# A two-layer encoder step on one core: stacked index queries, and attention and retention steps put in another order

## What is computed

```
qi = rope(qi) * IDX_DIM ** -0.5                      # 16 index heads of 64
s_idx = einsum('bqhd,bsd->bqhs', qi, ki)
s_idx = einsum('bqhs,bqh->bqs', relu(s_idx), wi)
sel   = top_k(where(admissible, s_idx, -inf), topk)
p = softmax(s); o = einsum('bqcgs,bqscd->bqcgd', p, v_sel)
# retention, per head, chunk by chunk
o = einsum('bihd,bjhd->bhij', q, k) * decay
o = einsum('bhij,bjhe->bihe', o, v) + einsum('bihd,bhde->bihe', q, s) * inter
od = rmsnorm(o, g_dn) * silu(dg)
```

## Time and profile before

| | us |
|---|---|
| median of 3 runs (2869.24 to 2869.51) | 2869.35 |
| the profiled execution | 2871.04 |
| its span, first to last instruction | 2869.1 |
| PE busy with matmuls in the span | 2851.2 |
| DVE, ACT, POOL busy | 1428.7, 1070.8, 186.4 |

### The profile page before, as it was taken

One profiled execution on the slowest core, in us unless ns is written; L12 is line 12 of the kernel. 1 busy time (PEld: TensorE's weight loads), 2 busy tenths in 40 slices (PEclk: granted clock), 3 DMA queues, 4 the chain that ended last, 5 costly groups with the idle time before them and its releaser, 6 DMA issues.

```text
span 2869.1 us, 45023 instructions
## 1 busy us (share of the span) xinstructions
PE 2851.2 (99%) x18666; PEld 2806.6 (98%) x18666; DVE 1428.7 (50%) x1546; ACT 1070.8 (37%) x1236; POOL 186.4 (6%) x112
## 2 busy tenths in 40 slices
PE   9999999999999999999999999999999999999999
PEld 9997799999999999999999999899999999999999
DVE  7677645543443343344466774546444443444443
ACT  5334533332332233233335633434333333333332
POOL 2000002000000000000221241112000000000000
PEclk9999999999999999999999999999999999999999
DMA  6433024444444444444444444244444444444443
GB/s 232 138 114 110 30 89 140 143 143 140 146 141 141 145 140 141 145 140 141 145 148 155 152 148 148 95 162 147 149 153 147 154 147 152 150 149 153 147 152 136
DMA packets 112783, 405.25 MB, mean 141 GB/s; under 512 B 12656, under 2 KB 14752, under 8 KB 112480
## 3 DMA queue, kind: packets, MB, share of 16 engines
q1 hardware_dynamic: 108864, 392.64, 41.1%
q0 software_dynamic: 1616, 6.31, 0.6%
q10 hardware_dynamic: 2128, 3.66, 0.3%
HBM read 396.48 MB, written 6.09 MB: 140 GB/s over the span
## 4 chain that ended last, share of the span: by engine, by line
PE 97%; DVE 2%; ACT 1%; issue 0%; DMA 0%; ACTq 0%; DVEq 0%
PE PS L1411 31%; PE PS L1416 30%; PE PS L1415 30%; PE PS L1490 0%; ACT pr L483 0%; DVE pr L910 0%; DVE w_lo L843 0%; PE PS L1691 0%; DVE rb L1052 0%; PE PS L1488 0%; PE PS L1866 0%; PE PS L1474 0%; ACT w_hi L435 0%; PE PS L1738 0%; PE PS L1737 0%
## 5 line engine op out<-in xcount | busy, mean ns | idle before, releaser
L843 DVE TENSOR_TENSOR w_lo<-stage,w_hi 128x1024 fp32r<-128x1024 f32 x734 | 920.3, 1256 | 1197.0 <-ACT w_hi L435 1196.6
L435 ACT ACTIVATE w_hi<-stage 128x1024 fp32r<-128x1024 f32 x740 | 784.6, 1061 | 1634.3 <-PE PS L1416 1624.9
L1411 PE MATMUL PS<-xh,w_hi 128*128 128x336 f32 (+1 forms) x3264 | 1025.1, 314 | 1.0 <-DVE kk L1087 0.6
L1416 PE MATMUL PS<-xh,w_lo 128*128 128x336 f32 (+1 forms) x3248 | 1017.1, 313 | 0.0
L1415 PE MATMUL PS<-xl,w_hi 128*128 128x336 f32 (+1 forms) x3248 | 1015.6, 313 | 0.0
L1411 PE MATMUL PS<-hh,w_hi 128*128 128x336 f32 (+1 forms) x2032 | 635.7, 313 | 0.0
L1416 PE MATMUL PS<-hh,w_lo 128*128 128x336 f32 (+1 forms) x2032 | 635.0, 313 | 0.0
L1415 PE MATMUL PS<-hl,w_hi 128*128 128x336 f32 (+1 forms) x2032 | 634.1, 312 | 0.0
L1411 PEld LDWEIGHTS PS<-xh,w_hi 128*128 128x128 f32 x3264 | 613.1, 188 | 3.5 <-issue 1.1
L1415 PEld LDWEIGHTS PS<-xl,w_hi 128*128 128x128 f32 x3248 | 612.5, 189 | 0.4
L1416 PEld LDWEIGHTS PS<-xh,w_lo 128*128 128x128 f32 x3248 | 610.0, 188 | 0.0
(11 more groups left out here) (343 smaller groups left out, 1529.1 us busy)
## 6 DMA issues: line engine op xcount, KB each, us to landing
stage<-in_wstream SPq DMA_DIRECT2D x740, 512.0 KB, 3.3
out_s<-so POOLq DMA_DIRECT2D x8, 256.0 KB, 2.8
x<-in_x_in SPq DMA_DIRECT2D x6, 336.0 KB, 7.1
out_y<-x ACTq DMA_DIRECT2D x3, 672.0 KB, 3.9
dmask<-in_ret POOLq DMA_DIRECT2D x4, 352.0 KB, 5.7
stage<-in_wstream SPq DMA_DIRECT2D x4, 256.0 KB, 3.7
s<-in_s_in POOLq DMA_DIRECT2D x1, 1024.0 KB, 6.2
x<-in_x_in SPq DMA_DIRECT2D x4, 168.0 KB, 3.9
```

What stands on the lines that cost most here:

```text
L435: act.activation(w_hi[:, s, :], stage[:, s, :], ACT.Copy).then_inc(hi_ready, 1)
L843: dve.tensor_tensor(w_lo[:, s, :], stage[:, s, :], w_hi[:, s, :].bitcast(F32), ALU.subtract).then_inc(lo_ready, 1)
L1411: pe.matmul(out, wh, rh, start=first, stop=False)
L1416: mm = pe.matmul(out, wl, rh, start=False, stop=last)
```

## The change

- **Index.** A head's 64 rows of rounded query and the rest of them now lie over each other in one 128-row tile (`qeven`, `qodd`). The keys' rounded part is in all rows, so one pass gives both products, and a second gives rounded query by low key: two passes, not three. ACT rounds into both tiles (four copies of 128x1344, two before), DVE writes the rest over the other head's rows (eight instructions of 32x1344, two of 128x1344 before).
- **Query projection.** The copy out of four banks becomes four copies of one bank, and PE waits for each by itself. The sums of squares start with the part of `sqq` that is there first.
- **Attention.** `pta` and `ptb` are both copied by ACT, ahead of the exponentials of the step. `mol` comes a step later. DVE makes the weights of heads 0 and 1 before it copies the sums. Half of a key unit moves ahead of the transposes of head 6.
- **Retention.** Outputs alternate between banks 6, 7 and 1, 2 (`out_bank`), squares between `osq` and `osq2`. DVE makes the decay mask before it waits for the root. ACT's rounding of output h - 1 (`round_output`) comes after the copies for head h + 1.

The core of the diff:

```diff
-        qih = place("qih", [P, 8, T], B + 20 * TB, F32R)
+        qeven = place("qeven", [P, 8, T], B + 20 * TB, F32R)
+        qodd = place("qodd", [P, 8, T], B + QI * TB, F32R)
         kph = place("kph", [P, 2, KEYS], B + 16 * TB, F32R)
...
+
+        def squares_of(h):
+            return osq2 if h % 2 else osq
+
+
+        def out_bank(h):
+            return 1 if h % 2 else 6
...
+                    if g0 == 0 and s == 8:
+                        softplus_input()
+                        act.wait_ge(qb_taken, 1)
+                        act.activation(sdq[0:8], sdq[0:8], ACT.Sqrt, bias=gcol("eps", rows=slice(0, 8))
+                                       ).then_inc(qb_sd, 1)
+                    if 2 <= s < 10:
+                        g = g0 + s - 2
+                        act.wait_ge(pt_psum, g + 1)
+                        if g >= 2:
+                            act.wait_ge(o_psum, g - 1)
+                        act.activation(pta[:, g % 2], PS[:, pb, :].rearrange("p (a b) -> p a b", a=4),
+                                       ACT.Copy).then_inc(pta_ready, 1)
+                        act.activation(ptb[0:80, g % 2, 0:80], PS[0:80, pb + 1, 0:80], ACT.Copy)
+                        act.activation(ptb[NS_TOK:80, g % 2, 80:T], PS[NS_TOK:80, pb + 1, 80:T],
+                                       ACT.Copy).then_inc(ptb_ready, 1)
...
-                    if 2 <= s < 10:
-                        g = g0 + s - 2
-                        act.wait_ge(pt_psum, g + 1)
-                        if g >= 2:
-                            act.wait_ge(o_psum, g - 1)
-                        act.activation(pta[:, g % 2], PS[:, pb, :].rearrange("p (a b) -> p a b", a=4),
-                                       ACT.Copy).then_inc(pta_ready, 1)
...
-                if (g, j) in ((2, 8), (3, 8)):
-                    act.wait_ge(qi_turned, g - 1)
-                    act.activation(qih[:, 4 * g - 8:4 * g - 4, :], zt4[:, g - 1], ACT.Copy).then_inc(qih_ready, 1)
...
+                for q, c, at_ in ((qeven, 0, (2, 8)), (qodd, 0, (2, 8)), (qeven, 1, (3, 8)), (qodd, 1, (3, 9))):
+                    if (g, j) == at_:
+                        act.wait_ge(qi_turned, c + 1)
+                        act.activation(q[:, 4 * c:4 * c + 4, :], rb4[:], ACT.Copy).then_inc(qih_ready, 1)
...
+            def round_output(h):
+                act.wait_ge(od_ready, h + 1)
+                act.activation(moh[:, 8 + 2 * h:10 + 2 * h, LIVE], z2[:, DG + 2 * h:DG + 2 * h + 2, LIVE],
+                               ACT.Copy).then_inc(doh_ready, 1)
...
                     tokens_first(h + 1)
+                if h:
+                    round_output(h - 1)
                 act.wait_ge(oms_psum, h + 1)
...
-                act.wait_ge(od_ready, h + 1)
-                act.activation(moh[:, 8 + 2 * h:10 + 2 * h, LIVE], z2[:, DG + 2 * h:DG + 2 * h + 2, LIVE],
-                               ACT.Copy).then_inc(doh_ready, 1)
+            round_output(3)
...
+                def weights(g):
+                    dve.wait_ge(p_ready, g + 1)
+                    ch.link(dve.reciprocal(rsum[:, g % 3, :], rsum[:, g % 3, :]))
+                    for q in range(3):
+                        seg = pr[:, g % 3, SEG[q]:SEG[q + 1]]
+                        e = dve.tensor_scalar(seg, seg, rsum[:, g % 3, q:q + 1], None, ALU.mult)
+                    e.then_inc(pn_ready, 1)
+
+                for s in range(8 + 4):
                     if s < 8:
...
+                    if 1 <= s < 9 and (g0, s) != (0, 2):
+                        weights(g0 + s - 1)
                     if g0 == 0 and s == 1:
+                        weights(1)
                         dve.wait_ge(qb_ms, 1)
-                        dve.tensor_copy(sdq[0:8], PS[0:8, 4:6, 0:T]).then_inc(qb_taken, 1)
-                    if 2 <= s < 10:
-                        g = g0 + s - 2
-                        dve.wait_ge(pt_psum, g + 1)
-                        if g >= 2:
-                            dve.wait_ge(o_psum, g - 1)
-                        dve.tensor_copy(ptb[0:80, g % 2, 0:80], PS[0:80, pb + 1, 0:80])
-                        dve.tensor_copy(ptb[NS_TOK:80, g % 2, 80:T], PS[NS_TOK:80, pb + 1, 80:T]).then_inc(ptb_ready, 1)
-                    if g0 == 0 and s == 9:
+                        dve.tensor_copy(sdq[0:8, 1], PS[0:8, 5, 0:T])
+                        dve.wait_ge(qb_ms, 2)
+                        dve.tensor_copy(sdq[0:8, 0], PS[0:8, 4, 0:T]).then_inc(qb_taken, 1)
+                    if s >= 4:
...
-                    if s >= 3:
-                        g = g0 + s - 3
-                        dve.wait_ge(moh_ready, g + 1)
-                        dve.tensor_tensor(mol[:, h0 + s - 3, :], PS[:, ob + g % 2, 0:T],
-                                          moh[:, h0 + s - 3, :].bitcast(F32),
-                                          ALU.subtract).then_inc(mol_ready, 1)
...
+                        dve.tensor_tensor(rb4[:], q4, rb4[:], ALU.add).then_inc(qi_turned, 1)
+
+                for c, odd, r, at_ in ((0, 0, 0, (2, 9)), (0, 0, 64, (2, 9)), (0, 1, 32, (2, 10)), (0, 1, 96, (2, 10)),
+                                        (1, 0, 0, (3, 9)), (1, 0, 64, (3, 10)), (1, 1, 32, (3, 11)), (1, 1, 96, (4, 4))):
+                    if (g, j) == at_:
+                        dve.wait_ge(qi_turned, c + 1)
+                        dve.wait_ge(qih_ready, 2 * c + 1 + odd)
+                        q8 = (qeven, qodd)[odd][:, 4 * c:4 * c + 4, :]
+                        to = r + 32 - 64 * odd
+                        dve.tensor_tensor(q8[to:to + 32], rb4[r:r + 32], q8[r:r + 32].bitcast(F32),
+                                          ALU.subtract).then_inc(qstack_ready, 1)
...
+                    ch.link(dve.tensor_tensor(kpl[:], kpad[:, 0:2, :], kph[:].bitcast(F32), ALU.subtract))
+                    dve.tensor_tensor(kph[:, 0], kph[:, 0].bitcast(F32), kph[:, 1].bitcast(F32),
+                                      ALU.add).then_inc(kpl_ready, 1)
...
-                if (g, j) == (7, 8):
+                if (g, j) == (7, 9):
...
-                    dve.tensor_copy(qb[:, 4 * c:4 * c + 4, :], PS[:, 4:8, 0:T]).then_inc(qkv_evac, 1)
+                    for o in range(4):
+                        dve.tensor_copy(qb[:, 4 * c + o, :], PS[:, 4 + o, 0:T]).then_inc(qkv_evac, 1)
...
+                if h < 3:
+                    decayed_scores(h + 1)
                 dve.wait_ge(osd_ready, h + 1)
                 ch.link(dve.reciprocal(osd[:, LIVE], osd[:, LIVE]))
-                if h < 3:
-                    decayed_scores(h + 1)
...
-                                qh, ql = qih[:, h // 2, t0:t0 + P], qil[:, h // 2, t0:t0 + P]
-                                pe.matmul(out, qh, kph[:, h % 2, k0:k1], start=True, stop=False)
-                                pe.matmul(out, qh, kpl[:, h % 2, k0:k1], start=False, stop=False)
-                                mm = pe.matmul(out, ql, kph[:, h % 2, k0:k1], start=False, stop=True)
+                                q_ = (qeven, qodd)[h % 2][:, h // 2, t0:t0 + P]
+                                pe.matmul(out, q_, kph[:, 0, k0:k1], start=True, stop=False)
+                                mm = pe.matmul(out, q_, kpl[:, h % 2, k0:k1], start=False, stop=True)
...
+                def bank_free(o):
+                    pe.wait_ge(qkv_evac, 4 * c - 3 + o)
...
-                pe.wait_ge(qb_sq, 3)
+                pe.wait_ge(qkv_evac, 10)
+                pe.wait_ge(qb_sq, 1)
...
+                    pe.wait_ge(qb_sq, 2 + j // 4)
...
-                   lambda s: keys_b(0) if s == 9 else None)
+                   lambda s: keys_b(0, range(2)) if s == 8 else None,
+                   lambda s: keys_b(0, range(2, 4)) if s == 9 else None)
...
+                if h >= 2:
+                    pe.wait_ge(on_ready, 2 * h - 2)
+                tb = out_bank(h)
...
-                    pe.wait_ge(on_ready, 2 * h)
-                else:
+                if h == 0:
                     pe.wait_ge(s0_in_s, 16)
+                pe.wait_ge(ktok_ready, h + 1)
                 pe.wait_ge(qd_ready, h + 1)
                 pe.wait_ge(pT_ready, h + 1)
...
```

More of the change, by code:

```diff
@@ L268, in build @@
         osd = place("osd", [P, T], B + 17408 + 2 * TB)
+        osq2 = place("osq2", [P, 2, T], A + 14 * TB)
         PS = ctx.enter_context(nc.psum_tensor("PS", [P, 8, 512], F32))
@@ L499, in attend @@
                                        ACT.Copy).then_inc(moh_ready, 1)
-                    if g0 == 0 and s == 8:
-                        softplus_input()
-                        act.wait_ge(qb_taken, 1)
-                        act.activation(sdq[0:8], sdq[0:8], ACT.Sqrt, bias=gcol("eps", rows=slice(0, 8))
-                                       ).then_inc(qb_sd, 1)
             def mlp(n, u_mlp, g_mlp, L, whole, ahead=None):
@@ L798, in _ @@
                 act.wait_ge(do_psum, h + 1)
-                act.activation(osq[:, :, LIVE], PS[:, 1:3, LIVE], ACT.Square).then_inc(osq_ready, 1)
+                b = out_bank(h)
```

(26 more changed lines are left out.)

76 lines of the change are left out of this document (35 added, 41 removed).

## The result

| | before | after |
|---|---|---|
| median of 10 runs, us | 2869.45 (2868.83 to 2870.89) | 2876.85 (2875.03 to 2879.09) |
| the profiled execution | 2871.04 | 2876.41 |
| its span | 2869.1 | 2874.6 |
| mean granted clock | 0.999 | 0.998 |
| PE busy with matmuls | 2851.2 | 2848.1 |

The changed kernel is 7.4 us slower by the medians, 0.26%; the ratio of the two is 1.002, with an interval of 1.0012 to 1.0028. So it is slower, by somewhat more than the 0.2% (5.7 us) that the prediction named as the least that can be told from no change. The forecast was 2873.5 with a range of 2865 to 2879.

A forecast was written before the change was run, and what follows sets the result against it. The prediction took PE to bound the kernel, busy 2851.2 of 2869.1 us. Index +1.9, attention A -4.2, attention B -1.3, retention +4.5 and clock +3.3 sum to +4.2 on 2869.35, so 2873.5 us, range 2865 to 2879.

The forecast's parts named there:

- two waits of 4.7: Retention, h = 1 and h = 2: PE idles 4.7 us from the transposes' end to the squares, +9.4 together.
- The rival without the stall: Retention: the sample state is read in time, term -4.9 instead of +4.5, two dips go, 2860.8; chance 0.13.
- The 0.2 that the sum adds to each wait for refilling: Attention and retention: each removed wait of PE also saves about 0.2 us in which PE's queue refills.
- a period falls from 5.85 to about 5.73: Index stage: the time from one pair of heads to the next shrinks only this far; six periods save 0.7 us.
- if PE's own work were the limit. It is not: Index stage: the loop outside PE limits the pairs, so the 5.7 us of matmuls saved over eight pairs isn't won.
- The rival of cheap subtractions and a limit at PE's work: Index stage: pairs shorten by their full 0.71, 32-row subtractions cost 0.4: -5.7 instead of +1.9, 2865.9; chance 0.12.
- a new wait of 3.3: Attention of A: the first transposes start where they did, so time saved ahead becomes some 3.3 us of PE waiting.
- the 4.2 of the sum: Attention of A: values of head 7 come 4.2 us earlier, 3.9 of waits plus 0.8 of refill less 0.5.
- the 0.45 of the sum: Attention of A, step 8: root and table load, 1.28 us, stand ahead of a `pta`; 0.45 of that is not covered.
- I take the two longest: Clock: of four new idle stretches (4.7, 4.7, 3.3, 2.9 us), two are followed by half clock, +3.3 us.
- took off 1.7 for the dip of before: Retention: the half-clock stretch behind the first wait for `osq` in the kernel before goes, -1.7 us.
- slower, by the clock: Rival: every long idle is followed by the 1.2 GHz level, two dips more, +3.4, so 2876.9; chance 0.33.

The follow-up runs named there:

- b_idx: Kernel before with only the index part of the change, the stacked index queries: 2872.03 us, ratio 1.0005.
- b_two_passes: Kernel before with two passes of the index scores, leaving out low query by rounded key: 2867.41 us, ratio 0.9988.
- b_att: Kernel before with only the parts of the change in query projection and attention: 2864.98 us, ratio 0.9983.
- b_one_pass: Kernel before with one pass of the index scores, rounded query by rounded key: 2864.70 us, ratio 0.9982.
- b_ret: Kernel before with only the retention part of the change: 2879.91 us, ratio 1.0033.
- idx_subs_behind: Changed kernel with the 32-row subtractions behind the additions of their step instead of ahead: 2873.37 us.
- att_weights_behind: Changed kernel with the weights of head 1 behind DVE's two copies of the sums of squares: 2875.18 us.
- ret_low_later: Changed kernel with DVE's low part of output h - 1 behind the sample state and decay mask of head h: 2864.15 us, ratio 0.9975.
- all_three: Changed kernel with DVE's low part later, subtractions behind additions, head 1's weights behind the copies, and ACT's last query rounding ahead of the ReLUs: 2855.78 us, ratio 0.9947.

## Why the prediction was right, and where it was not

The measured time lies in the range, but outside the 2869 to 2876 that the forecast kept for itself: +7.4 is in the part that was called slower, with a chance of 0.35. The waits and the order behind them came as described. Two errors on the clock, both the same way, make the rest, and that the number stayed in the range owes something to the width of the range.

- **Retention, the wait.** Forecast: two waits of 4.7 through copies, rounding, `mol` and `so`. Measured: 4.57 each, in that order, and 4.6 with the part alone. Moving one DVE instruction took both away. The rival without the stall, 0.13, is out. The 0.2 that the sum adds to each wait for refilling, for which it shows no row, comes out too: 13.5 us less in the stage for 13.1 of waits and half clock, and 0.19 behind the wait of pair 2 (7.53 between the pairs, less 5.07 and 2.27).
- **Index stage.** Forecast +1.9, measured +1.7, with 2.3 and 2.8 of new waits where 2.1 (by the start of pair 2) and 2.9 were expected. Of the 1.7, 0.3 lies ahead of pair 0, which starts at 116.93 and not 116.66, after a wait of 0.6 for `xl` at 13.8 us, far ahead of the stage; from pair 0 on it is +1.5, in `b_idx` too. Two sizes inside were off and cancelled, which is luck: chunk 4 came 3.5 late and not 2.9, and the pairs behind it gave back 1.8 and not 1.0, since the loop's period was put at 5.73 and is 5.48 on the mean. The step "a period falls from 5.85 to about 5.73" took one pass through the loop for the steady state. And "if PE's own work were the limit. It is not" holds for the changed kernel only: in the kernel before PE had no wait for `rt`, and its own work filled the 5.85. The price of the 32-row subtraction, 1.55, was exact, so the number of rows does not count in it:

```profile
124.65 1.55 DVE L1128 TENSOR_TENSOR qeven<-rb,qeven 32x1344 fp32r<-32x1344 f32 x1
```

  The rival of cheap subtractions and a limit at PE's work, -5.7, is out; of its saving in PE's work about half came (3.0 of 5.7 in `b_two_passes`).
- **First transposes.** Forecast: they start where they did before, a new wait of 3.3. Measured: 283.17, which is 281.44 plus the 1.7 that the index stage brought, and a wait of 2.8.
- **The steps of attention.** From first transposes to the values of head 7 it was 31.66 us and is 28.84, less by 2.8. With the half-clock stretch of 282.8 to 286.2 in it (some 1.5 of matmul time) that is 4.3 against the 4.2 of the sum. Mixer B gave 1.5 against 1.3. Two rows of ACT in the changed kernel, the table load ahead of the root and the two `ptb` copies, show the sizes:

```profile
303.95 1.28 ACT L490 ACT_TABLE_LOAD   x1
305.25 0.85 ACT L490 ACTIVATE sdq<-sdq,gains 8x672 f32<-8x672 f32 x1
...
306.49 0.21 ACT L499 ACTIVATE ptb<-PS 80x80 f32<-80x80 f32 x1
306.71 0.37 ACT L500 ACTIVATE ptb<-PS 16x256 f32<-16x256 f32 x1
```

  The copies are 0.6 together, where 0.8 was taken between 0.5 and 1.2. The load with its root ends at 306.10, and PE waits 0.57 for `ptb` of that step, against the 0.45 of the sum. The root starts 0.02 behind the load; the drain of the Trainium skill (ScalarE: Activation LUTs, section What ACT_TABLE_LOAD costs) shows neither in the rows nor in the wait.
- **The clock was mis-sized.** The sum took two dips, +3.3. The profile has four lengths of the dip of the earlier trace rows at the 1.2 GHz level, 3.4 + 6.8 + 3.4 = 13.7 us; less the 2.7 in which PE stood idle anyway (282.8 to 283.2, 1825.6 to 1827.7, 1846.1 to 1846.3), half of the rest is 5.5 us. The step "I take the two longest" failed twice: the first wait of retention was followed by two lengths, and the wait of 2.8 by one.
- **And it was booked against the wrong number.** The sum took off 1.7 for the dip of before and carried the result to the median. But the profiled execution of before was 1.7 above the median because of that dip, and the profiles of `b_idx`, `b_att` and `b_one_pass`, with the same retention code, have none there. Without it before's profile would stand at 2869.3, where the median is. The executions of before beside the experiments say the same: the 36 with a granted clock of 1.000 have medians of 2869.4 to 2869.6 in the three series, the 30 with 0.999 have 2871.4 to 2872.1. So the median's execution most likely has no dip, and there was nothing to take off. Without any dip before's span would be 2869.1 - 1.7 = 2867.4 and the changed kernel's 2874.6 - 5.5 = 2869.1: +1.7 from waits and matmuls (the sum's own terms without clock are 1.9 - 4.2 - 1.3 + 9.4 - 3.2 = +2.6), and +5.5 from the clock. These make +7.2, against the +7.4 of the medians.
- So the median landed on the number of the rival "slower, by the clock" (2876.9, chance 0.33), though not by its book, and that is luck as well: it wanted one dip behind each of four waits, and the profile has none in the index stage.

The Trainium skill (TensorE: Matmul & The Clock Gate, section HAM oscillation — how this bites in real kernels) has a PE put back to half clock by a long wait between bursts of matmuls, so that the next burst starts cold. The runs agree for the longest waits: in the changed kernel, in `b_ret`, `idx_subs_behind` and `att_weights_behind` the clock is at half for 3.4 to 6.8 us behind each of the two waits of 4.6. Behind the shorter ones, for which that section names no such fall, it came too, but not every time. The wait of 2.8 at the first transposes was followed by a dip in the changed kernel, `b_att` and `idx_subs_behind`, and by none in `ret_low_later`. In the index stage it is the other way round: a dip in `ret_low_later`, `b_idx` and `att_weights_behind`, none in the changed kernel. In retention, where before's code waits 1.4 twice, there is a dip in before and in `b_two_passes`, none in `b_idx`, `b_att` and `b_one_pass`. What decides in the shorter ones stays open; no experiment was made for it.

## What to carry to other kernels

When an instruction is moved behind others on one engine, go through what already stands behind its consumer on the next engine: here ACT's rounding went behind six copies, and a DVE instruction (at 1826.17) whose result PE takes up some 30 us later (the last projection starts at 1858.09) held up one that PE needed at once. On a kernel that is bound by PE, work without a deadline belongs behind, not ahead of, the short instruction that frees a bank; a handful of such moves turned +7.4 us into some -14. And before an effect of the clock is put into a sum, ask whether the runs of the median have it at all.

## What the runs showed of the hardware

- Idle PE costs more than the idle time. The edit in retention took 9.1 us of waits away and brought 12.7 by the medians, 13.5 in the stage itself, where half clock accounts for 4.0; all edits of `all_three` took 9.1 + 1.3 + 4.5 = 14.9 us of waits away, and brought 21.1.
- The same code with the same waits had its dip at different places from profile to profile, and the time of one kernel can spread by it: 2875.03 to 2879.09 for the changed kernel, with granted clocks of 0.996 to 0.998, but 2855.62 to 2856.94 for `all_three`, whose five executions all have 1.000. It need not: `b_ret`, with 10.3 us of half clock in its profile, stayed within 2879.59 to 2880.17. One dip is 3.4 us at half clock, and costs up to 1.7.
- A subtraction over 32 partitions took as long as one over 128, 1.55 us for 1344 elements a row (124.65 in the changed kernel, before).
